# Sample attention of a decode step: scores and weighing in four column groups, cached pages loaded under other conditions

## The reference

```python
full_slc = pad_rows(concatenate([cache_kv_slc[page_table].reshape(past_shape), new_slc], axis=1), SEL_BLOCK)
kv_win_all = concatenate([state_kv_win, new_win], axis=1)
...
s = einsum('btgrd,bsgd->btgrs', q_rot, kv[:, :, 0]) * ATTN_SCALE     # 4 key heads g, 4 queries r each, head size 64
p = masked_softmax(s, mask)
o = einsum('btgrs,bsgd->btgrd', p, kv[:, :, 1])
```

## Time and profile before

| what | value |
|---|---|
| time, median of 3 runs | 1646.98 us (1646.54 to 1647.13) |
| profiled execution | 1645.52 us, of which the span is 1643.3 us |
| PE busy | 1608.2 us (98%) |
| DVE, ACT, POOL busy | 848.8, 560.9, 93.2 us |
| sample attention | from 1121.9 us to the first `out_first` at 1184.2 us |

### The profile page before, as it was taken

How to read it: one execution, slowest core, us unless ns; L and a number is a source line. 1 busy time by engine, 2 the same in 40 slices (tenths; PEclk the granted TensorE clock), 3 DMA queues, 4 the chain that set the end, 5 groups by cost and what they waited for, 6 DMA issues and landing times.

```text
span 1643.3 us, 31449 instructions
## 1 busy us (share of the span) xinstructions
PE 1608.2 (98%) x12978; PEld 1497.3 (91%) x12978; DVE 848.8 (52%) x1322; ACT 560.9 (34%) x957; POOL 93.2 (6%) x154
## 2 busy tenths in 40 slices
PE   7999999999999999999999989998999999999998
PEld 6999999999999999999998757676699999999998
DVE  5228753365444434445165689986465544524433
ACT  6335221233221112134343667675453212112111
POOL 0000000000000000000000035551000000000000
PEclk9999999999999999999999999999999999999999
DMA  5257221323223232222244423003542232322312
GB/s 161 78 169 264 74 72 59 113 83 91 89 77 102 77 89 90 82 73 77 81 135 130 128 95 99 15 2 114 145 114 92 78 102 77 101 79 77 103 58 74
DMA packets 135279, 156.74 MB, mean 95 GB/s; under 512 B 11290, under 2 KB 119122, under 8 KB 134770
## 3 DMA queue, kind: packets, MB, share of 16 engines
q1 hardware_dynamic: 135106, 155.42, 30.1%
q10 hardware_dynamic: 80, 0.02, 0.0%
HBM read 149.58 MB, written 14.16 MB: 100 GB/s over the span
## 4 chain that ended last, share of the span: by engine, by line
PE 92%; DVE 3%; ACT 3%; issue 1%; DMA 0%; POOL 0%; SPq 0%; DVEq 0%; ACTq 0%
PE PS L653 62%; PE PS L683 12%; PE PS L1115 2%; PE PS L1032 2%; PE PS L1130 2%; PE PS L835 1%; PE PS L690 1%; PE PS L1185 1%; PE PS L995 1%; PE PS L1087 1%; PE PS L1220 1%; PE PS L1098 1%; PE PS L698 1%; PE PS L1170 1%; DVE hst L2255 1%
## 5 line engine op out<-in xcount | busy, mean ns | idle before, releaser
L653 PE MATMUL PS<-act0h,wh 128*128 128x272 f32 x1664 | 345.1, 288 | 0.0
L653 PE MATMUL PS<-act0l,wh 128*128 128x272 f32 x1664 | 343.8, 288 | 0.0
L653 PE MATMUL PS<-act0h,wl 128*128 128x272 f32 x1664 | 343.7, 288 | 0.0
L1355 ACT ACTIVATE wh<-raw 128x2048 fp32r<-128x2048 f32 x106 | 203.0, 1915 | 408.8 <-PE PS L653 408.7
L1791 DVE TENSOR_TENSOR wl<-raw,wh 128x2048 fp32r<-128x2048 f32 x106 | 243.1, 2293 | 170.0 <-ACT wh L1355 169.9
L653 PEld LDWEIGHTS PS<-act0h,wh 128*128 128x128 f32 x1664 | 260.2, 188 | 0.5
L653 PEld LDWEIGHTS PS<-act0l,wh 128*128 128x128 f32 x1664 | 260.1, 188 | 0.0
L653 PEld LDWEIGHTS PS<-act0h,wl 128*128 128x128 f32 x1664 | 260.1, 188 | 0.0
L1824 DVE TENSOR_TENSOR hT<-PS,hT 128x544 f32 (+1 forms) x72 | 52.1, 724 | 209.8 <-PE PS L653 209.7
L683 PE MATMUL PS<-wh,act0h 128*128 128x256 f32 x448 | 129.3, 289 | 0.0
L683 PE MATMUL PS<-wh,act0l 128*128 128x256 f32 x448 | 125.7, 281 | 0.0
(11 more groups left out here) (328 smaller groups left out, 2485.9 us busy)
## 6 DMA issues: line engine op xcount, KB each, us to landing
raw<-in_ffn_w_gate SPq DMA_DIRECT2D x44, 512.0 KB
raw<-in_ffn_w_up SPq DMA_DIRECT2D x44, 512.0 KB
raw<-in_a_w_in SPq DMA_DIRECT2D x32, 512.0 KB
raw<-in_ffn_w_down SPq DMA_DIRECT2D x32, 512.0 KB
raw<-in_a_w_out SPq DMA_DIRECT2D x16, 512.0 KB
crows<-in_cache_kv_cmp SPq DMA_DIRECT2D x32, 256.0 KB, 2.9
cache<-in_cache_kv_slc SPq DMA_DIRECT2D x32, 256.0 KB, 4.3
cache<-in_state_kv_win SPq DMA_DIRECT2D x8, 1024.0 KB, 8.0
```

Of the source, the lines that this page charges most:

```text
L653: mm = pe.matmul(PS[:, 4 * ps + 2 * mt + h, 0:HALF], W[:, rs, k, mt * P:mt * P + P], Xp[:, k * T + h * HALF:k * T + h * HALF + HALF], star ...
L1355: act.activation(wh[:, rs, :, :], raw[:, rs, :, :], ACT.Copy).then_inc(w_hi, 1)
```

## The change

Scores: the four pairs of sample and half, (s, p), get 32 PSUM rows each, with their own 32 query columns; the halves are no longer added. Weighing: the same four groups of 32 rows, each against its own 128 value channels, so twice as many matmuls of half the width. The result has 128 columns, its copy to `od` is 128 wide and `d_back` has one transpose. Loads: places 4 and 5 are swapped in memory; sample 4 is loaded when three quarters of the head pairs of prompt attention are weighed, sample 5 when all prompt scores are made, and when prompt attention is done, the pages of sample 6 go to a spare half place; at `d_o` = 1 only the window of sample 6 and all of sample 7 are issued.

```diff
     slots = [at(f"cache{j}", a, [P, 2, PAGES, 512])
-             for j, a in enumerate((A_WH, A_WL, A_RAW, A_P2 + 30720, A_P2 + 30720 + 16384, A_P2 + 8192))]
+             for j, a in enumerate((A_WH, A_WL, A_RAW, A_P2 + 30720, A_P2 + 8192, A_P2 + 30720 + 16384))]
+    spare = at("spare", A_P0 + 11264, [P, PAGES, 512])
+    IN_SPARE = len(slots)
+    def cached(b, br):
+        return spare if (b, br) == (IN_SPARE, 0) else slots[b % len(slots)][:, br]
+    def loaded_by(b):
+        first = 16 * (PAGES + 1)
+        return kv_load[b % len(slots)], first + (0 if b < len(slots) else 16 if b == IN_SPARE else first)
...
         def sample(b):
             j = b % len(slots)
-            pages(slots[j][:, 0], cache_kv_slc, b, kv_load[j])
+            if b != IN_SPARE:
+                pages(slots[j][:, 0], cache_kv_slc, b, kv_load[j])
...
         sample(3)
+        sp.wait_ge(a_o, 2 * LAST_TILE)
+        sample(4)
+        sp.wait_ge(a_s, WSTEPS + PAIRS - WIDE)
+        sample(5)
         sp.wait_ge(a_o, HALVES)
-        for b in range(4, 6):
-            sample(b)
+        pages(spare, cache_kv_slc, IN_SPARE, s_spare)
         sp.wait_ge(d_o, 1)
...
         def d_keys(b):
-            C = slots[b % len(slots)]
-            pe.wait_ge(kv_load[b % len(slots)], 16 * (PAGES + 1) * (b // len(slots) + 1))
+            pe.wait_ge(*loaded_by(b))
+            if b == IN_SPARE:
+                pe.wait_ge(s_spare, 16 * PAGES)
...
         def d_scores(bp):
-            both = [(2 * bp + s, slice(64 * s, 64 * s + 64)) for s in range(2)]
+            four = [(2 * bp + s, p, slice(64 * s + 32 * p, 64 * s + 32 * p + 32), slice(32 * p, 32 * p + 32))
+                    for p in range(2) for s in range(2)]
...
-                for p in range(2):
-                    for b, rows in both:
-                        pe.matmul(PS[rows, 4 + br, :], Qbd[:, 1, p, b, :], KTd[b % 2][:, br, p, :],
-                                  start=(p == 0), stop=(p == 1))
-                for p in range(2):
-                    for b, rows in both:
-                        pe.matmul(PS[rows, 6, br * TD:br * TD + TD], Qbd[:, 1, p, b, :], knT[:, br, p, :],
-                                  start=(p == 0), stop=(p == 1))
+                for b, p, rows, own in four:
+                    pe.matmul(PS[rows, 4 + br, :], Qbd[:, 1, p, b, own], KTd[b % 2][:, br, p, :], start=True, stop=True)
+                for b, p, rows, own in four:
+                    pe.matmul(PS[rows, 6, br * TD:br * TD + TD], Qbd[:, 1, p, b, own], knT[:, br, p, :], start=True, stop=True)
...
+            for b, p, rows, own in four:
+                mm = pe.matmul(PS[rows, 6, 2 * TD:2 * TD + NCMP], Qbd[:, 0, p, b, own], kcr[:, 1 + b, p, :],
+                               start=True, stop=True)
...
         def d_weigh(bp):
-                    for C, rows in both:
-                        pe.matmul(PS[rows, 7, 0:256], PTd[:, 4 * br + pg, rows], C[:, br, pg, 256:512],
+                    for s, C, rows, e in four:
+                        pe.matmul(PS[rows, 7, 0:P], PTd[:, 4 * br + pg, rows], C[br][:, pg, 256 + e:256 + e + P],
                                   start=(br == 0 and pg == 0), stop=False)
...
-            for p in range(2):
-                tr = pe.transpose(PS[:, 7, 256 + P * p:256 + P * p + P], od[:, P * p:P * p + P], ident)
-            tr.then_inc(d_ot, 1)
+            pe.transpose(PS[:, 7, 256:256 + P], od[:, 0:P], ident).then_inc(d_ot, 1)
...
-            act.activation(od[:, :], PS[:, 7, 0:256], ACT.Copy).then_inc(d_oe, 1)
+            act.activation(od[:, 0:P], PS[:, 7, 0:P], ACT.Copy).then_inc(d_oe, 1)
```

More of the change, by code:

```diff
@@ L313, in build_program @@
     kv_load = [sem(f"sample_cache{j}") for j in range(6)]
+    s_spare = sem("sample_cache_spare")
     d_tr, d_kd, d_ka = sem("sample_keys_transposed"), sem("sample_keys_dve"), sem("sample_keys_act")
@@ L1169, in d_keys @@
                     for pg in range(PAGES):
-                        tr = pe.transpose(PS[:, 2 * br + p, pg * P:pg * P + P], C[:, br, pg, P * p:P * p + P], ident)
+                        tr = pe.transpose(PS[:, 2 * br + p, pg * P:pg * P + P], C[:, pg, P * p:P * p + P], ident)
                     tr.then_inc(d_tr, 1)
         def d_scores(bp):
-            both = [(2 * bp + s, slice(64 * s, 64 * s + 64)) for s in range(2)]
+            four = [(2 * bp + s, p, slice(64 * s + 32 * p, 64 * s + 32 * p + 32), slice(32 * p, 32 * p + 32))
+                    for p in range(2) for s in range(2)]
             if bp >= 1:
@@ L1182, in d_scores @@
                 pe.wait_ge(d_ka, 4 * bp + br + 3)
-                for p in range(2):
-                    for b, rows in both:
-                        pe.matmul(PS[rows, 4 + br, :], Qbd[:, 1, p, b, :], KTd[b % 2][:, br, p, :],
-                                  start=(p == 0), stop=(p == 1))
-                for p in range(2):
-                    for b, rows in both:
-                        pe.matmul(PS[rows, 6, br * TD:br * TD + TD], Qbd[:, 1, p, b, :], knT[:, br, p, :],
-                                  start=(p == 0), stop=(p == 1))
-            for p in range(2):
-                for b, rows in both:
-                    mm = pe.matmul(PS[rows, 6, 2 * TD:2 * TD + NCMP], Qbd[:, 0, p, b, :], kcr[:, 1 + b, p, :],
-                                   start=(p == 0), stop=(p == 1))
+                for b, p, rows, own in four:
[5 more added lines that the diff above has]
+                               start=True, stop=True)
             mm.then_inc(d_s, 1)
@@ L1214, in d_weigh @@
                 pe.wait_ge(d_oh, 4 * bp)
-            both = [(slots[(2 * bp + s) % len(slots)], slice(64 * s, 64 * s + 64)) for s in range(2)]
+            four = [(s, [cached(2 * bp + s, br) for br in range(2)], slice(64 * s + 32 * p, 64 * s + 32 * p + 32), P * p)
+                    for p in range(2) for s in range(2)]
             for br in range(2):
@@ L1224, in d_weigh @@
                 c0 = 512 * (1 + br) + 256
[L1225 to L1228, removed]
+                for s, C, rows, e in four:
+                    pe.matmul(PS[rows, 7, 0:P], PTn[:, br, rows], kvtok[0:TD, QT, c0 + e:c0 + e + P], start=False, stop=False)
+            for s, C, rows, e in four:
+                mm = pe.matmul(PS[rows, 7, 0:P], PTn[0:NCMP, 2, rows], vc[:, 1 + 2 * bp + s, e:e + P], start=False, stop=True)
             mm.then_inc(d_o, 1)
@@ L1331, in head_psum @@
     def head_psum(p, g2):
-        v = PS[64 * g2:64 * g2 + 64, 7, 256 + P * p:256 + P * p + P].rearrange("q (s x) -> q s x", s=2)
+        v = PS[64 * g2:64 * g2 + 64, 7, 256:256 + P].rearrange("q (s x) -> q s x", s=2)
         return v[:, :, 32 * p + 16 * g2:32 * p + 16 * g2 + 16].rearrange("q s (r t) -> q s r t", r=R)
```

1 line of the change is left out of this document (added).

## The result

The changed kernel takes 1630.71 us (median of 4 runs, 1628.25 to 1632.14) against 1646.76 us of the kernel before, measured beside it (4 runs, 1644.3 to 1647.13): 16.05 us less, a ratio of 0.9905 with the interval 0.9884 to 0.9926. The forecast itself as a ratio, 0.9922, is just inside the interval, so the medians alone hardly refute it. The step of the forecast that failed is the length of ACT's queue in turns 0 and 1: from a weighing to the next scores it gave 8.14 us, and it is 7.62 and 7.53, which with the scores makes 1.4 us more than forecast in the two turns. The traces show that, and also that a part of the 16 us does not come from the sample attention at all.

What follows compares the result with a forecast made beforehand. PE, busy 98% of the span, was taken as the bound. Terms -4.14 - 3.07 - 3.1 - 0 - 2.38 - 0.11 = -12.8 us gave 1634.2 us against the median; 8-in-10 range 1632.0 to 1640.0 us.

Steps and rivals of the forecast that it cites:

- turns 0 and 1: First two weighings up to the next ones: ACT's queue becomes the bound; savings of 3.07 and 3.1 us.
- Four groups at once: Scores and weighing on PE: four column groups run together, saving 2.07 us per scores and 2.38 us per weighing.
- the six small steps: Small score products: twelve pairs become six steps of unchanged length, saving 0.35 us per scores (bounds 0 to 0.52).
- The start: First keys to first weighing: scores 0 and scores 1 each shorten by 2.07 us, together -4.14 us.
- Instructions bound the weighing: Rival: doubled records at 0.058 us keep a weighing near 5.1 us; 1638.6 us in all, chance 0.07.
- w + 8.14 us: Start of the next scores, counted from the weighing's start w, by ACT's summed copies; 9.14 us before.
- Turn 2: Third weighing to last turning: path of 6.39 us, none of it PE's, so the saving is 0.
- the last two terms: Fourth weighing directly before `out_first`, -2.38 us, and the single transpose in `d_back` ahead of the output projection, -0.11 us.
- The clock: Rival: PE's new gaps lower the granted clock; low throughout or another loss had chance 0.05.
- The long fall: Clock low from the first gap to the output projection: 21.4 us lost, 1655.6 us; chance 0.05 with other losses.
- The short fall after weighing 2: One brief clock drop in PE's gap there, costing some 2.5 us, 1636.7 us; counted within the forecast's 0.80.
- The loads: Samples 4 and 5 beside prompt attention cost 0 us (bounds 0 to 0.3 each); sample 7 hidden, 2 us to spare.

Runs made afterwards that it cites:

- e2: The changed kernel run again for a second profile, no edit: 1630.41 us, ratio 0.9900 to the kernel before.
- e7: The kernel before with only the new loads; scores, weighing and `d_back` as before: 1645.91 us, ratio 0.9997.
- e10: The changed kernel with key copies ahead of `od`, key transposes ahead of `d_back`, and filler transposes around the third `d_back`: 1628.40 us, ratio 0.9897.
- e8: The changed kernel with 11 and 4 unread filler transposes in PE's waits after the third weighing: 1627.86 us, ratio 0.9882.
- e5: The kernel before with scores and weighing both in four groups, all loads as before: 1641.02 us, ratio 0.9962.
- e12: e10 with 8 more filler transposes behind the keys of sample 3, before the second scores: 1629.35 us, ratio 0.9897.
- e3: The kernel before with only the scores in four groups; weighing and loads as before: 1643.61 us, ratio 0.9981.
- e4: The kernel before with only the weighing in four groups, its narrow copy and single transpose; scores and loads as before: 1646.75 us, ratio 1.0004.
- e1: The kernel before run again for its profile, no edit: 1643.94 us (one run).

## Why the prediction came out as it did

**Four groups at once: right.** Steps of 0.43 us, scores 2.04 us (2.18 forecast), weighing 2.67 (2.67). The 0.14 in the scores is the six small steps, which cost less than the unchanged step that I took and lie within the bound that I gave. The start, turn 0 and turn 1 thus saved a little more; the start 4.4 us instead of 4.14 (19.46 to 15.05 us from the first keys to weighing 0, by e2).

**Instructions bound the weighing: wrong.** 64 records at 0.030 each, the pace of the small score products, not the 0.058 of the earlier trace rows. The figure of about 62 ns a matmul that the Trainium skill gives in "TensorE: Matmul & The Clock Gate", the section on the gap of 56 ns, holds by its own words with hardware decoding off; a weighing of 5.5 us was the estimate by it. The trace shows 88 records in 2.67 us, so it does not bind here, and no run shows which way the decoding is set.

**Turns 0 and 1: the step that failed, a term that was mis-sized.** The forecast put weighing to scores at w + 8.14 us, and it is 7.62 and 7.53. I had seen rightly that ACT becomes the bound, and the order of its queue. The timeline of the changed kernel, engine ACT, in turn 0, whose weighing starts at 1138.76:

```profile
1143.55 0.22 ACT L1756 ACTIVATION_READ_ACCUMULATOR PD<-PS,small 128x1 f32 x1
1143.64 0.29 ACT L1771 ACTIVATE od<-PS 128x128 f32<-128x128 f32 x1
1143.80 1.11 ACT L1748 ACTIVATE KTb<-PS 128x512 f32<-128x512 f32 x2
1144.75 0.86 ACT L1779 ACTIVATE oT<-PS 64x32 f32<-64x32 f32 x4
1145.64 1.28 ACT L1748 ACTIVATE KTd<-PS 128x512 f32<-128x512 f32 x2
```

Each starts before the one ahead of it has ended: `od` has a duration of 0.29 us, but the next copy starts 0.16 after it; the two key copies last 1.11 and hold the queue for 0.95. I had added durations, 0.3 + 1.21 + 0.83 + 0.60, and come to w + 8.14; by starts it is 4.88 for `od`, 5.04, 5.99, 6.88 for the copy of sample 5, and the scores at 7.62. In turn 1 it is 7.53. From weighing to weighing that gives 11.19 and 11.10 us: 3.7 and 3.8 us saved instead of 3.07 and 3.1. (By the forecast's own sum it was 11.86 and 11.8; the 12.0 that it gives as a sign and uses for the loads does not agree with its -3.07.) Near the rows that I used the kernel before shows it too, where the copies to `oT` start at 1148.92, 0.49 us after this one:

```profile
1148.43 0.60 ACT L1734 ACTIVATE KTb<-PS 128x512 f32<-128x512 f32 x1 [0.28 <-PE PS L1170]
```

**Turn 2 and the last two terms: right.** From weighing 2 to the last turning 6.38 us (6.39), and from `out_first` to the first full item 14.43 against 14.53: -0.10 (-0.11). Turn 3 saves its 2.4 us where the clock stays.

**The clock: a rival that was right in its small form.** The long fall, which would have made the kernel slower, did not come. The short fall after weighing 2, priced at 2.5 us inside the forecast, came in every trace with the short weighing and no fillers and costs 1.4; further stretches in some executions bring it to 4.2. It follows gaps of 2.4 and 0.9 us, where the row on which I had leaned shows 1 us of one with 1.00.

**The loads: right for what was asked, not for why it matters.** The cost is zero (e7) and in the changed kernel the keys of sample 7 follow the first `d_o` after 1155.26 - 1141.43 = 13.8 us with no wait; I had 12.7 for the loads and 15 for the keys, so by that estimate 1.1 us were left where I had counted on 2. Even that is too much: in e10, which wants these keys earlier, PE waits for the load until 13.38 us behind `d_o` = 1. The line of e10, engine PE:

```profile
1151.37 0.86 PE L1190 MATMUL PS<-cst,cache 128*128 128x128 f32 x5 [0.28 <-DMA cache<-in_state_kv_win]
```

So by this trace some 0.4 us are left in the changed kernel, an estimate (13.83 - 13.38): a turn shortened by more would meet the load. But the sentence that the old order needs 17 us is wrong in a faster kernel: it needs 19.8 to 21.1, as the output weights then fall into it. In the medians the effect of both parts together is three times that of the groups alone (16 us against 4.8), in the stage about twice. With the old loads, the step sum for the groups would have been 8 us off.

**The sum.** Where the clock stays up, the stage saves 4.4 + 7.6 + 0 + 2.4 + 0.1 = 14.5 us, as e8 shows. The forecast had 12.8: 0.3 too little in the start and 1.4 in turns 0 and 1. The changed kernel loses 1.4 to 4.2 of the 14.5 to the clock, so its stage saves 10.3 and 13.0 in the two profiles. That the second comes within 0.3 us of the forecast's 12.8 is luck: the mis-sized turns and the clock nearly cancel there. The profiled spans of before and changed differ by another 3.0 us: 2.1 by the pace of the feed-forward and 0.9 before the stage, where the clock is low for 10.2 us near 900 in the kernel before and for 3.4 in the changed one. Over all 14 traces the stage starts at 1122.5 us on average where that stretch is 10.2 us long (5 traces, e5 and e12 with the new groups among them) and at 1120.4 where it is 3.4 (8 traces, e3 and e4 with the old loads among them). So both occur with old and with new code. The mean granted clock of every execution is on record too: of the 52 executions of the kernel before that were measured beside e1 to e12, 10 have 0.997 or more, where the two profiled ones, with the long stretch, have 0.995, and the median of these 10 is 1644.1 us against 1645.8 of all. So the kernel before has executions with less low clock as well, and they are some 1.7 us faster. I can't show that the medians are free of it: whether executions of the kernel before fall into the long stretch or the slower pace more often than those of the changed kernel stays open, and with it the 2 to 6 us by which the differences of the medians (16.1 and 15.3) go beyond those of the stage (10.3 and 13.0).

## What to carry to other kernels

When one engine of a chain gets faster, look at what it triggers: a semaphore that comes earlier can put a transfer that nobody is waiting for into the way of one that somebody is, and then the faster version gains little until the loads are moved too. Test both halves alone and together. Build the new wait of a queue from the distances between the starts of its instructions, not from their durations. A matmul product whose stationary side is block-diagonal over heads wastes half of two groups of 64; as four groups of 32 it costs half, as long as the doubled number of records (0.030 us each here) still fits into the time of the columns.

## What the runs showed of the hardware

- Four column groups with stationary 32 wide, float32: a group of four with 512 moving columns takes 0.43 us, 16 groups with 128 moving columns take 1.96 us, the tail included.
- In e5 the DMA engines moved 374 GB/s at a share of 1.02 from 1154 to 1156 us, and 211 and 187 at 1.1 in the 4 us after that, with the output weights among the transfers.
- The granted clock fell to 0.50 in 6 of 6 traces behind a gap of PE of 2.4 us, a transpose and 0.9 us more, and in none of 4 in which transposes of a constant filled most of it. It fell at the same place in e3 too, behind waits of 0.48 and 0.34 us with which three other traces kept 1.00. Near 900 us the same instructions ran at 0.50 for 3.4, 6.8 or 10.2 us in different executions.
- The same float32 matmuls at a granted clock of 1.00 run at two paces that hold for a whole execution, 1591 and 1602 records in 200 us, in executions of the same program. What sets it is not known.
